# Streaming encoder on one core: the three terms of a weight product, column half by column half

## The reference

```python
for layer in range(2):
    h = h + 0.5 * swiglu_ffn(h, ffn1_g, ffn1_w_in, ffn1_w_out)   # 1024 -> 2 x 2816 -> 1024
    hn = rmsnorm(h, mix_g)
    if layer == 0:
        y, S = retention_mixer(hn, S0, pos, chunk_len, ret_w_in, ret_gn_g, ret_w_out)  # 4 heads
    else:
        y = fox_mixer(hn, fox_w_q, fox_w_out, k_all, v_all, ...)  # 16 heads
    h = h + y
    h = h + 0.5 * swiglu_ffn(h, ffn2_g, ffn2_w_in, ffn2_w_out)
    if layer == 0:
        k_new, v_new, logf_new = fox_kv(h, kv_g, w_kvf, b_f)
return rmsnorm(h, final_g), S, k_new, v_new, logf_new            # for prompt and sample
```

## Time and profile before

| | us |
|---|---|
| median of 3 runs | 2575.29 |
| lowest and highest | 2573.64, 2575.78 |
| the profiled execution, its own time | 2575.13 |
| span of the profiled execution, first to last instruction | 2573.2 |
| TensorE busy | 2534.7 |
| its weight loads busy | 2463.8 |
| VectorE busy | 1057.4 |
| ScalarE busy | 694.6 |
| GpSimd busy | 344.2 |

### The profile page before, as it was taken

How to read it: one execution, slowest core, us unless ns; L and a number is a source line. 1 busy time by engine, 2 the same in 40 slices (tenths; PEclk the granted TensorE clock), 3 DMA queues, 4 the chain that set the end, 5 groups by cost and what they waited for, 6 DMA issues and landing times.

```text
span 2573.2 us, 44082 instructions
## 1 busy us (share of the span) xinstructions
PE 2534.7 (99%) x18791; PEld 2463.8 (96%) x18791; DVE 1057.4 (41%) x1556; ACT 694.6 (27%) x990; POOL 344.2 (13%) x273
## 2 busy tenths in 40 slices
PE   9999999999999999999999999999999999999998
PEld 8999999989898979999999999999998789999998
DVE  4332334553635465332334333323335654332333
ACT  4221222222213222221222232212223542221221
POOL 0100113120101012100113221100121022100112
PEclk9999999999999999999999999999999999999999
DMA  5232233222222122232332432322233422232231
GB/s 150 82 102 62 85 93 89 75 78 74 87 67 90 54 66 83 82 102 63 89 94 72 140 104 85 96 82 74 86 86 107 116 78 82 82 101 63 82 96 48
DMA packets 393653, 221.71 MB, mean 86 GB/s; under 512 B 8032, under 2 KB 385984, under 8 KB 393520
## 3 DMA queue, kind: packets, MB, share of 16 engines
q1 hardware_dynamic: 388688, 205.13, 27.6%
q0 software_dynamic: 4640, 14.58, 1.7%
q10 hardware_dynamic: 192, 0.04, 0.0%
HBM read 206.01 MB, written 13.71 MB: 85 GB/s over the span
## 4 chain that ended last, share of the span: by engine, by line
PE 96%; DVE 2%; ACT 1%; issue 0%; DMA 0%; SPq 0%; POOL 0%; ACTq 0%; DVEq 0%; POOLq 0%
PE ps L1508 87%; PE ps L1887 1%; PE ps L1691 1%; PE ps L1677 1%; PE ps L1679 1%; PE ps L1678 1%; DVE wl L589 1%; PE ps L1915 1%; PE ps L1939 1%; PE ps L1711 0%; DVE xl L899 0%; PE ps L1792 0%; PE ps L1670 0%; DVE h L944 0%; DMA xtok<-in_x_sample 0%
## 5 line engine op out<-in xcount | busy, mean ns | idle before, releaser
L589 DVE TENSOR_TENSOR wl<-raw,wh 128x1024 fp32r<-128x1024 f32 (+3 forms) x352 | 450.8, 1281 | 1280.0 <-ACT wh L584 1280.0
L1508 PE MATMUL ps<-xh,wl 128*128 128x288 f32 x4000 | 861.7, 297 | 5.2 <-DVE xl L899 2.7
L1508 PE MATMUL ps<-xh,wh 128*128 128x288 f32 x4000 | 853.4, 295 | 0.0
L1508 PE MATMUL ps<-xl,wh 128*128 128x288 f32 x4000 | 853.1, 295 | 0.0
L584 ACT CAST wh<-raw 128x1024 fp32r<-128x1024 f32 (+3 forms) x352 | 375.9, 1068 | 1158.9 <-PE ps L1508 1158.0
L1508 PEld LDWEIGHTS ps<-xh,wl 128*128 128x128 f32 x4000 | 643.0, 189 | 11.5 <-issue 3.9
L1508 PEld LDWEIGHTS ps<-xh,wh 128*128 128x128 f32 x4000 | 643.3, 189 | 0.0
L1508 PEld LDWEIGHTS ps<-xl,wh 128*128 128x128 f32 x4000 | 643.3, 189 | 0.0
L1508 PE MATMUL ps<-actl,wh 128*128 128x288 f32 x1408 | 301.1, 295 | 0.0
L1508 PE MATMUL ps<-acth,wl 128*128 128x288 f32 x1408 | 301.0, 295 | 0.0
L1405 POOL TENSOR_TENSOR rsilu<-silu,rstd 128x576 f32<-128x576 f32 x88 | 125.9, 1430 | 1294.9 <-ACT silu L637 1294.9
(11 more groups left out here) (248 smaller groups left out, 1663.4 us busy)
## 6 DMA issues: line engine op xcount, KB each, us to landing
raw<-in_ffn_w_in SPq DMA_DIRECT2D x176, 512.0 KB, 3.8
raw<-in_ffn_w_out SPq DMA_DIRECT2D x32, 768.0 KB, 4.8
raw<-in_ret_w_in SPq DMA_DIRECT2D x48, 512.0 KB, 3.8
raw<-in_ffn_w_out SPq DMA_DIRECT2D x32, 640.0 KB, 4.3
raw<-in_ret_w_out SPq DMA_DIRECT2D x32, 256.0 KB, 2.7
raw<-in_fox_w_kvf SPq DMA_DIRECT2D x16, 512.0 KB, 4.1
raw<-in_fox_w_q SPq DMA_DIRECT2D x8, 512.0 KB, 4.8
bias<-cum_scratch SPq DMA_DIRECT2D x16, 256.0 KB, 3.4
```

The lines of the kernel that those rows point to most:

```text
L589: nc.vector.tensor_tensor(wl[:, s % SPLIT, 0:kt, :], raw[:, s, 0:kt, :], wh[:, s % SPLIT, 0:kt, :].bitcast(F32), ALU.subtract).then_inc(lo ...
L1508: mm = nc.tensor.matmul(out[:, a:z], w, x[:, a:z], start=start and n == 0, stop=stop and n == len(terms) - 1)
```

## The change

The two loops of `product` change places. Before, each term is done for both halves of the columns before the next term; now, all three terms are done for the first half, and then all three for the second. The operands, the number of instructions and the start and stop marks of each half stay the same.

```diff
@@ product @@
-                for n, (w, x) in enumerate(terms):
-                    for a, z in CUTS:
+                for a, z in CUTS:
+                    for n, (w, x) in enumerate(terms):
                         mm = nc.tensor.matmul(out[:, a:z], w, x[:, a:z],
                                               start=start and n == 0, stop=stop and n == len(terms) - 1)
                 return mm
```

## The result

The changed kernel takes 2589.94 us (median of five runs, 2587.53 to 2591.00), the kernel before 2575.06 beside it (2573.38 to 2575.78). The ratio is 1.0059, with a 95% interval of 1.0046 to 1.0072: 0.6% slower. The profiled execution took 2589.94 us, its span is 2588.0.

A forecast was written before the change was run, and what follows sets the result against it. TensorE's step between products was taken to bound the kernel. Waits, same-bank adds, weight changes and rhythm, each 0 us, summed to 0 against the profiled 2575.1, giving 2575 us; range 2541 to 2610.

The forecast's parts named there:

- the fast stretches lose their rhythm: Rival: second parts' input products, 3840 matmuls, fall from 130.0 to 133.3 ns; +12.7 us, 2588 us, chance 0.14.
- What bounds the kernel: Whole kernel: TensorE, busy 99% of the span, sets the end by its step from one product to the next.
- One price for each class: Matmul classes: 3840 at 130.0 ns, 8160 at 133.3, 5280 at 132.2, each kept through the program; sum 2285 us.
- Waits, 0 us: Block starts and unit signals: same first and last product in both orders, so the 13.7 us of waits stay; 0 us.
- (a): Products inside a half: adding to the same bank and columns twice in a row carries no penalty; 0 us.
- The sign that the prediction named for such a penalty: At 288 columns, the two steps inside a half would be longer than the one between halves; no size given.
- (b): Each block: two more changes of weights, four instead of two; taken as 0 us, upper bound +38.5 us.
- that rival: Every change of weights costs 6.7 ns, two more per block: +38.5 us, 2614 us, chance 0.19.
- (c): All 288-column products: which rhythm the new order falls into; taken as 0 us, between -38.5 and +12.7 us.

The follow-up runs named there:

- `TURN_HALF`: Kernel before, in1 input sections alone reading halves a b, b a, a b over the three terms, weights changing as before: 2588.50 us beside 2574.30.

## Why the prediction was wrong

The forecast was no change, 2575 us; measured is +14.9. The time is inside the range, the direction is not the forecast's. The rival "the fast stretches lose their rhythm", 2588 us, is what happened.

- **What bounds the kernel**: right. TensorE's steps are the time, and the whole change is in them.
- **One price for each class**: right, from one stretch each. All four in1 sections were fast and all four in0 slow, in the windows above and in the one at 1765 us (x772, x752 with that section tipped). The exceptions are the three single units of the retention heads at 130.0, worth 0.5 us.
- **Waits, 0 us**: right, 13.6 against 13.7.
- **(a) The same bank and columns twice in a row, 0 us**: right, and more firmly than the retention heads could say: with every product of the old order in one bank, on the same columns, the steps are the same as with two. The sign that the prediction named for such a penalty did show faintly: averaged over the starts from 280 to 370 us after, the steps inside a half are 133.8 ns and those between halves 132.5. But the mean of the six, 133.3, is that of the old order's slow stretches, whose steps differ among themselves as well (131.3 within a pair, 135.4 from pair to pair, 80 to 160 us before).
- **(b) Changes of weights, 0 us**: right. Four per block at 130.0 ns in the run with alternating halves; that rival is refuted.
- **(c) The rhythm, taken as 0 us**: this step failed. Its bound from above, "the fast stretches fall to 133.3: 3840 x 3.3 = +12.7 us", is the value. The reason I gave for 0 was that "the number of instructions, the widths and the ratio of loads to products, which a rhythm would follow, are untouched". The runs show a rhythm that follows something else: in which order the two halves of the moving tile are read, and what ran before. With `TURN_HALF`, those numbers and the weights' changes are all as before, and the rhythm is lost.
- The prediction said that the rival had against it that "nothing in a section decides for it that I could find". That was the clue, read the wrong way. Two identical pieces of code at two speeds were, in this kernel, a state that is handed on, and such a state can be held by one order and not by another. A rival with that clue for it deserved more than the 0.14 I gave it.

What is shown: the loss is in the in1 sections; alternating halves allow 130.0, other orders tried do not; neither the PSUM bank (tried with the old order) nor the changes of weights matter; the old order runs in either rhythm; one block, or eight, tipped a stretch at 130.0 ns in twelve tests of twelve at the end, and one block tipped some stretches at 133.3 ns. What stays open: why alternating reads of the moving tile permit the shorter step; where in the hardware the state lies, how many states there are, which slow stretch a block will tip, and why 132.2 ns with acth/actl; and about 1 us of the 14.8.

## What to carry to other kernels

When the same code runs at two speeds in one trace, suspect a state that is entered and handed on, and look for what enters it before pricing any reordering: count instructions in equal windows of every section, since busy shares don't show it. Where a tile is cut into column halves, try first to keep the halves alternating; here 2.5% of a step hung on it, and changes of weights cost nothing. An odd block that helps where it stands must be judged over the sections behind it too, because they are entered from another state.

## What was unexpected of the hardware

- A stream of 128x288 products with a load each has two stable steps on xh/xl, 130.0 and 133.3 ns, 2.5% apart, in the same code at full clock. Six products in another order, 0.8 us of work, can switch it for the 100 us and more behind, and not every slow stretch is switched.
- The switch outlives a section of other operands that itself steps at 132.2 ns both times.
- The slow step of the new order and the slow step of the old one look alike (133.3 ns), but 48 old-order products of acth/actl turn the one into slow again and the other into fast.
- Reading one half alone gives a third step, 131.8 ns.
- Writing every product into one PSUM bank costs nothing (133.1 and 130.0 ns against 133.1 and 129.9 with two), and four changes of weights per block cost nothing against two.
- The fast step is 130.0 / 288 = 0.451 ns per column.
